# A streaming-encoder step: later tiles' queries in one pass beside tile 0's experts, short loads reordered

## What is computed

```python
h   = RMSNorm(x)
z   = h @ w_in     # q/k/v of two attentions, forget logits f, two gates: 6664 columns
o_A = DiffAttn(q_A, k_A, v_A)                      # 8 heads, two maps each
o_B = FoX(q_B, k_B, v_B, cumsum(log_sigmoid(f)))   # 8 heads, decay by C[t] - C[s]
x   = x + (sigmoid(g_A) * (o_A @ w_pa) + sigmoid(g_B) * (o_B @ w_pb)) @ w_o
# PEER: q = RMSNorm(x) @ wq; top 16 of 128 x 128 product keys in each of 8 heads
x   = x + sum over 128 experts e of: softmax_weight * gelu(u[e] . xn) * v[e]
y   = RMSNorm_final(x)
```

## Time and profile before

| | us |
|---|---|
| median of 3 runs | 2085.18 |
| lowest and highest | 2084.87, 2090.12 |
| the profiled execution | 2091.16 |
| its span, first to last instruction | 2089.4 |
| first gather starts | 367.8 |
| last gather starts | 2059.1 |
| PE busy | 1615.2 (77%) |
| DVE busy | 1505.3 (72%) |
| POOL busy | 748.5 (36%) |
| ACT busy | 540.9 (26%) |
| gathers, software queue q0 | 570.46 MB, 67.1% of the DMA engines' span |
| SP's loads, q1 | 155.19 MB, 19.9% |
| ScalarE's saves and loads, q10 | 26.73 MB in 22512 packets, 3.7% |

### The profile page before, as it was taken

One profiled execution on the slowest core, in us unless ns is written; L12 is line 12 of the kernel. 1 busy time (PEld: TensorE's weight loads), 2 busy tenths in 40 slices (PEclk: granted clock), 3 DMA queues, 4 the chain that ended last, 5 costly groups with the idle time before them and its releaser, 6 DMA issues.

```text
span 2089.4 us, 22180 instructions
## 1 busy us (share of the span) xinstructions
PE 1615.2 (77%) x7119; PEld 1017.9 (49%) x7119; DVE 1505.3 (72%) x3453; ACT 540.9 (26%) x1429; POOL 748.5 (36%) x697
## 2 busy tenths in 40 slices
PE   7988899798877877989778767868886755666655
PEld 5778785375445724764466323535673222222211
DVE  1011219688887686889876999878688899988886
ACT  3242212111731221247402325732022210100111
POOL 0000000555443333234423444334255544555552
PEclk9998999999998988999889989988998878888888
DMA  7832774999999999999999989998999999999996
GB/s 229 303 116 77 270 242 139 393 421 419 424 420 421 421 376 400 381 396 358 361 398 420 409 348 396 361 399 337 421 404 421 397 398 421 396 422 421 422 408 265
DMA packets 129396, 753.80 MB, mean 361 GB/s; under 512 B 16992, under 2 KB 33296, under 8 KB 42880
## 3 DMA queue, kind: packets, MB, share of 16 engines
q0 software_dynamic: 78336, 570.46, 67.1%
q1 hardware_dynamic: 28432, 155.19, 19.9%
q10 hardware_dynamic: 22512, 26.73, 3.7%
HBM read 732.32 MB, written 19.48 MB: 360 GB/s over the span
## 4 chain that ended last, share of the span: by engine, by line
PE 36%; DMA 25%; DVE 24%; issue 8%; ACT 5%; ACTq 1%; POOL 1%; another core or an unknown queue 0%; SPq 0%; DVEq 0%; POOLq 0%; PEldq 0%
DMA ring<-in_uv,stage 19%; PE pz L1341 9%; DVE ring L2096 8%; PE acc L1681 7%; PE pz L1330 7%; DVE vsum L2123 5%; DMA wbuf<-in_w_q 2%; PE ps L1639 2%; PE ps L1602 1%; PE ps L1582 1%; DMA wbuf<-in_w_o 1%; DVE diag L2107 1%; DMA wbuf<-in_w_pa 1%; DMA zt<-F 1%; PE po L1424 1%
## 5 line engine op out<-in xcount | busy, mean ns | idle before, releaser
L876 POOL DMA_INDIRECT ring<-in_uv,stage x544 | 689.4, 1267 | 946.3 <-DVE vsum L2123 356.1
L1681 PE MATMUL acc<-ring,diag 128*128 128x512 f32 (+1 forms) x1068 | 599.5, 708 | 266.2 <-DVE diag L2107 208.3
L2096 DVE CUSTOM_DVE_ANT_0 ring<-ring,xb 128x1024 f32<-128x1024 f32 x544 | 650.5, 1222 | 93.9 <-DMA ring<-in_uv,stage 90.8
L1681 PEld LDWEIGHTS acc<-ring,diag 128*128 128x128 f32 (+1 forms) x1068 | 216.3, 216 | 611.4 <-DVE diag L2107 302.9
L2123 DVE SCALAR_TENSOR_TENSOR vsum<-ring,coefd,vsum 128x1024 f32<-128x1024 f32 x272 | 349.9, 1286 | 9.9 <-DVE coefd L2114 0.2
L1205 ACT ACTIVATE gel<-dots 128x1 f32<-128x1 f32 x544 | 103.6, 201 | 901.7 <-DVE dots L2096 897.5
L896 POOL COPY stage<-idx 128x4 int32<-128x4 int32 x136 | 56.3, 414 | 364.3 <-DVE gw L2042 363.5
L1330 PE MATMUL pz<-F,wbuf 128*128 128x128 f32 (+1 forms) x896 | 168.4, 346 | 7.6 <-PE pz L1330 4.6
L1330 PEld LDWEIGHTS pz<-F,wbuf 128*128 128x128 f32 x896 | 138.3, 194 | 38.0 <-issue 15.5
L2114 DVE TENSOR_SCALAR coefd<-gel,gw 128x1 f32<-128x1 f32 x277 | 58.2, 210 | 79.1 <-ACT gel L1205 78.7
L1205 ACT ACT_TABLE_LOAD x63 | 80.8, 1283 | 24.2 <-DVE xb L2163 16.3
(11 more groups left out here) (401 smaller groups left out, 1953.0 us busy)
## 6 DMA issues: line engine op xcount, KB each, us to landing
wbuf<-in_w_z SPq DMA_DIRECT2D x58, 1024.0 KB
wbuf<-in_w_q SPq DMA_DIRECT2D x32, 1024.0 KB
wbuf<-in_w_pa SPq DMA_DIRECT2D x16, 1024.0 KB
wbuf<-in_w_o SPq DMA_DIRECT2D x16, 1024.0 KB
ring<-in_uv,stage POOLq DMA_INDIRECT x544
wbuf<-in_w_pb SPq DMA_DIRECT2D x16, 512.0 KB
wbuf<-in_w_sk SPq DMA_DIRECT2D x4, 1024.0 KB
zt_mid<-F ACTq DMA_DIRECT2D x18, 128.0 KB
```

The source lines that it names most:

```text
L876: pool.indirect_dma_start(out=ring[:, slot, :], out_offset=None, in_=d["uv"], in_offset=bass.IndirectOffsetOnAxis(ap=stage[:, a, k:k + 1], ...
L1681: last = nc.tensor.matmul(acc[0:nq, c * 512:(c + 1) * 512], diag[:, parity, 0:nq], ring[:, slot, D + c * 512:D + (c + 1) * 512], start=Fal ...
L2096: nc.vector.tensor_tensor_reduce(out=u, in0=u, in1=xb[:, t % 2, :], scale=1.0, scalar=0.0, op0=ALU.mult, op1=ALU.add, accum_out=dots[:, sl ...
```

## The change

- Groups 4 and 5 are gone: queries of tiles 1 to 4 are passes of group 1 (416 tokens). They stand at the head of the work beside tile 0's experts; one (qa0) is ahead of the first expert slot.
- `EARLY` is 5: the head now holds f, ka0, ka2, ka4, ka6 of group 1. f stands at `NORM_X`, where a query pass of tile 1 stood; the last gate pass stands behind `NORM_O` instead of ahead of it. VectorE's part of the forget gate (at ka0) comes ahead of the selection.
- Tile 1's experts have the eight gate passes beside them and no query passes.
- SP issues norm1's gain first, with a semaphore of its own, then the weights of f and qa0, and then the ten other short loads. VectorE's copy of rel_bias moves behind the first transposes.
- The sample's attention has a class of its own in `ON_VECTOR`: 5 of 8 slots beside it are added on VectorE, where it was 3. In all tiles together 280 rows are added on VectorE, where it was 277 (85, 65, 64, 51, 15 by tile; before 80, 70, 61, 51, 15).

Cut to its core:

```diff
-QUERY_GROUPS = {4: (1,), 5: (2, 3, 4)}
-KEPT, KEPT_Q = 3, 5
+KEPT = 3
-EARLY = 3
-Q_ASKED = KEY_ITEMS[EARLY + 2]
+EARLY = 5
+Q_ASKED = KEY_ITEMS[-3]
@@ weight_of
-        return 11.5 if i == 1 else 4.6
+        return 9.0 if i == 1 and p in QUERY_ITEMS else 11.5 if i == 1 else 6.5
@@ make_plan
-                            for g, items in ((2, GATE_ITEMS), (4, QUERY_ITEMS), (1, KEY_ITEMS[:EARLY])))
-    beside_front = {NORM_O: queries[:1], NORM_X: queries[1:2],
+                            for g, items in ((2, GATE_ITEMS), (1, QUERY_ITEMS), (1, KEY_ITEMS[:EARLY])))
+    beside_front = {NORM_O: gates[-1:], NORM_X: keys[:1],
...
-        ahead = [("project", 1, i) for i in KEY_ITEMS[EARLY:]] if t == 0 else []
+        ahead = queries + [("project", 1, i) for i in KEY_ITEMS[EARLY:]] if t == 0 else []
         if t == 1:
-            ahead = [("project", KEPT_Q, i) for i in QUERY_ITEMS] + [("project", KEPT, i) for i in GATE_ITEMS]
+            ahead = [("project", KEPT, i) for i in GATE_ITEMS]
@@ beside
-            out[at] = stage = "turn" if p >= S_NORM else "attend"
+            out[at] = stage = "turn" if p >= S_NORM else "sample"
-ON_VECTOR = {"project": (0, 1, 2, 3, 4, 5, 6, 7), "attend": (1, 3, 6), ...
+ON_VECTOR = {"sample": (0, 1, 3, 4, 6), "project": (0, 1, 2, 3, 4, 5, 6, 7), "attend": (1, 3, 6), ...
@@ SyncE
-            sp.dma_start(hot, d["hot"]).then_inc(hot_landed, 16)
-            sp.dma_start(rb, d["rel_bias"]).then_inc(hot_landed, 16)
...
-                sp.dma_start(colg1[:, :], ...).then_inc(small_landed, 16)
+                sp.dma_start(colg1[:, :], ...).then_inc(g1_landed, 16)
+            def load_small():
...
             for n, (kind, piece) in enumerate(WEIGHTS):
+                if n == 2:
+                    load_small()
@@ ScalarE, turn_h and the pass of f
-                    act.wait_ge(small_landed, 16 * 9)
+                    act.wait_ge(g1_landed, 16)
...
+                        else:
+                            act.wait_ge(small_landed, 16 * 8)
@@ ScalarE, saving the queries of group 1
-                            act.dma_start(zt_mid[1:3, :, k0, :].rearrange("t p q -> p t q"),
-                                          dst[:, 0, 0:2 * P].rearrange("p (t q) -> p t q", q=P)).then_inc(z_saved[b], 16)
-                            act.dma_start(zt[TILES - 1][:, k0, :], dst[:, 0, 2 * P:n]).then_inc(z_saved[b], 16)
+                            act.dma_start(zt_mid[:, :, k0, :].rearrange("t p q -> p t q"),
+                                          dst[:, 0, 0:3 * P].rearrange("p (t q) -> p t q", q=P)).then_inc(z_saved[b], 16)
+                            act.dma_start(zt[TILES - 1][:, k0, :], dst[:, 0, 3 * P:n]).then_inc(z_saved[b], 16)
```

More of the change, by code:

```diff
@@ L220, in make_plan @@
                     YPROJ + 2: [("turn_h", 4, 0), ("keep_h", 1, 0)]}
-    for n, part in enumerate(spread(gates, lambda e: 1.0, NORM_O)):
+    for n, part in enumerate(spread(gates[:-1], lambda e: 1.0, NORM_O)):
         beside_front[n + 1] = part + beside_front.get(n + 1, [])
-    for n, part in enumerate(spread(queries[2:] + keys, lambda e: 11.8 if e[1] == 1 and e[2] else 5.0, PIECES - SCORE)):
+    for n, part in enumerate(spread(keys[1:], lambda e: 1.0, PIECES - SCORE)):
         beside_front[SCORE + n] = part
@@ L722, in query_group_of @@
         def query_group_of(t):
-            return next((g for g, group in QUERY_GROUPS.items() if t in group), 0)
+            return group_of(t)
         def group_cols(g):
```

48 lines of the change are left out of this document (25 added, 23 removed).

## The result

Four runs of the changed kernel took 2110.06 to 2122.43 us, median 2115.16, beside four of the kernel before with a median of 2087.65: ratio 1.0131, 95% interval 1.0110 to 1.0153. A second set of six, taken later as a control, gave 2113.44 against 2087.02: ratio 1.0116, interval 1.0089 to 1.0142. The prediction was 2084 with a range to 2098. Its profiled execution took 2110.06 us (span 2108.3), 18.9 more than the profiled one of before; the control's took 2122.70 (31.5 more).

The account below looks back on a forecast made before the run. Transfers (DMA share 1.00) were taken to bound most of the experts' part, with TensorE near its limit. Terms -3.2 + 22 - 18 - 2 = -1.2 gave 2090.0 profiled, less 6.0 for the median: 2084.0 us, range 2068 to 2098.

Parts of the forecast that it names:

- Tile 0, +22 predicted: Tile 0's experts: six added query passes and their saves lengthen the stage by 22 us, bounds 16 and 30.
- the attention of tile 1 then has eight slots fewer: Rest of tile 0's experts: tile 1's attention in fewer slots costs nothing extra, since VectorE has room (222 of 282.6 us busy).
- bytes and packets 21.1: Tile 0's experts: 10.0 us for weight bytes of added passes plus 11.1 for 6144 save packets; lower bound 16.1.
- The two agree: Tile 0's passes: TensorE's 168.8 us of passes end at 548, the transfers' 184.5 us at 549, both full.
- Head, -3.2 predicted: Start to first gather: the head's changes together bring the first gather from 367.8 to 364.6 us.
- -2.5 + 1.5 = -1.0: Before the output projection: short loads reordered give -2.5 us; the last gate pass behind NORM_O costs +1.5, bounds 0 and 3.
- +6.0: At NORM_X: f's pass and its ScalarE functions delay the copies that product-key queries wait for, 271.9 to 277.9 us.
- -8.2: Selection before the first gather: VectorE's forget-gate part moves into its 40.7 us wait for scores, saving 8.2 us.
- Tile 1, -18 predicted: Tile 1's experts: without six query passes VectorE sets the pace, 102.9 us instead of 120.9; bounds -26 and -3.4.
- rival 2: Tile 1's passes: VectorE's gelu waits stay at 22.6 us, the stage gives only 3.4, total 2098.6 us; chance 0.18.
- The sample's attention, -2: Sample's attention: three more rows added on VectorE shorten the chain through TensorE by 2 us, bounds -5.7 and +3.5.
- The signs given in advance: Signs of error: gather at 367 or later; in tile 0 TensorE awaiting weights or ScalarE saves; tile 1 gelu waits over 15.

## Why the prediction was wrong

The median came 31 us above the forecast. 20.0 of them are stages of the profiled execution, and 11.1 are the step from it to the median: before, the profile lay 6.0 above the median, and the prediction took that off; the changed kernel's lay 5.1 below its own. That step had one profile behind it, of a kernel whose executions lie between 2083 and 2095 us.

**Tile 0, +22 predicted, +31.5.** Two steps failed. The larger is "the attention of tile 1 then has eight slots fewer; VectorE is busy 222 of 282.6 us there and can take it": that stretch took 7.1 us more, at a seam of the plan where two heavy steps stood side by side. An average of busy time does not see this; the order of the program, which was at hand, does. The other is a size. From the first gather to slot 52 the prediction had bytes and packets 21.1 and "I add 1" for hitches; it measured 24.4. Over slots 0 to 52 the bytes alone are 19.8, where the prediction had 16.1, and the lower rate is 6.1, of which fewer packets gave 4.4 back. The packets' price was near the mark as a share of the engines (11.1 predicted; 6.2% of 173.1 us is 10.7 for all of ScalarE's queue there, before 1.3% of 148.0, 1.9, so 8.8 more), but it did not show as a lower rate while they passed. "TensorE: ... The two agree" counted a second limit that was only near: half its work in the query passes moved slots 0 to 52 by +1.1 us with the saves as they were and by -1.4 with merged ones.

**Head, -3.2 predicted, +1.7.** By places:

| | predicted | measured |
|---|---|---|
| up to the output projection | -2.5 + 1.5 = -1.0 | -0.7 |
| from there to the first MAX8 | +6.0 | +9.9 |
| from there to the first gather | -8.2 | -7.5 |

The first row is right by luck: the short loads alone bring 4 to 8 us up to there in three profiles, not 2.5, and some 5 are lost again where +1.5 was predicted, 1 of them by the missing pass at NORM_O, the rest for a cause that stays open. The failed step is in the second row. The forecast let f's pass stand where a query pass had stood, and had no term for TensorE's clock behind it: TensorE then waited 4.73 us, and the next pass took 6.57 us instead of 3.84. That is 2.7 of the 9.9; the other 7.2 stand against +6.0. At NORM_O the recorded sentence is "The query pass that stood there (3.8 us) was hidden in this; taking it away gives nothing." Nothing is what it gave on the path, and it took the clock there as well. The table loads took 1.28 us with no drain, as the rows of before had them. By the Trainium skill ("ScalarE: Activation LUTs", What ACT_TABLE_LOAD costs) with its 2.66 us for a switch the term would have been 8.8; the copies came 6.5 later, so the trace does not bear that out.

**Tile 1, -18 predicted.** -17.9 in the profiled execution, -8.3 in the control: the first is a hit by the luck of the execution. The "8 us" of kept waits for gelus were 7.9 there. In eight profiles of twelve they were 16 to 19, mostly with gate saves that landed late: that is rival 2's mechanism past its point of "about 15 us", with two thirds of its price (9.6 of 14.6 us in the control). The prediction gave it 0.18 and treated it as one of two outcomes; it is a thing that differs from one execution to the next. The two profiles with nine staging buffers did not have it, which is too few to call it shown.

**The sample's attention, -2.** Not to be seen in either direction; the stage varies by more.

**The signs given in advance.** A first gather at 367 or later, ScalarE waiting for saves in tile 0, and, in the control, gelu waits over 15 us in tile 1: three of the four came true. None of the rivals had tile 0 above +22; the term's own upper bound of 30 was passed by 1.5.

## What to carry to other kernels

A piece of work that is hidden in a wait may be what keeps TensorE at 2.4 GHz: before it is moved away, look at the granted clock of the next pass, and price that pass at the lower clock (here 6.3 to 6.8 us instead of 3.8). Where the DMA share is 1.00, count the bytes that must pass in the stretch first: here moving saves to another issuer, giving them buffers or spacing them only changed who waited, and fewer packets gave 4.7 of 25.9 us. When a plan spreads the same steps over fewer slots, read the new order for places where two heavy ones have come together, rather than comparing sums of busy time. And compare kernels stage by stage over several profiles: one profile each would have called tile 1's term a hit and missed it in the control.

## What was not expected of the hardware

A DMA issue on ScalarE, 0.38 us as a rule, took 5.11 and 7.88 us (14.4 in one run) while the transfer engines were full, and everything behind it in that queue waited. In tile 0's passes saves of 192 KB landed after 17.4 us in the median, while weight pieces of 1 MB on SP's queue took 9.1; one of the small zt_joint saves took 32.7 (in the run with the forget gate moved back). Profiles of one and the same kernel lie 12.6 us apart, and the long form of tile 1's passes is 8.6 of these. The head's second pass takes 3.84 us in seven of the seventeen profiles with the short loads in the new order and 5.2 to 6.6, at the lower clock for a part, in the other ten, so the first attention scores come anywhere between 96.5 and 101.7 us (before, in one profile, 102.2). The changed kernel's first profile, with 97.2, was among the lucky ones.
